# Gated DeltaNet stage: the order of work in its projection loop, and block products of 64x64 and 32x32 in two merge levels

## Chip, core and metric

The kernel runs on one core of a Trainium2 chip. The metric is the device time of one launch in microseconds (us). A core has a matrix engine (TensorE, "PE"), a vector engine (VectorE, "DVE"), a scalar engine (ScalarE, "ACT"), GpSimd ("POOL") and a queue engine (SyncE, "SP") that issues most loads. Each runs its own program in order; they meet at semaphores. PE writes to PSUM, eight banks of 128 partitions by 512 fp32.

## What is computed

Two decoder layers on 256 tokens of width 1024. Each layer is an FFN, a token mixer and a second FFN, so there are six stages: FFN, sliding-window attention, FFN, FFN, gated DeltaNet, FFN. The change is in the fifth. Cut to what matters, it is:

```python
q, k, v = split(silu(causal_depthwise_conv(qkv, conv_w)))     # 8 heads of 128
# per chunk, with gcum the running sum of the log decay
decay = exp(where(causal, gcum[..., :, None] - gcum[..., None, :], -inf))
a_mat = eye + where(strict, (k @ k.T) * decay * beta[..., :, None], 0)
sol   = triangular_solve(a_mat, concat([v * beta, k * beta * exp(gcum)]), lower=True)
v_new = u - w @ state                                         # u, w = split(sol)
out   = (q * exp(gcum)) @ state + where(causal, (q @ k.T) * decay, 0) @ v_new
```

The kernel uses chunks of 128 tokens, two of them, and inverts the unit triangular 128x128 matrix of each head and chunk: 16 matrices.

## The kernel before

**Stages and units.** Weights come in units of 2048 fp32 per partition. SP loads a unit into one of three slots, ACT rounds it to a high part (`hi`), DVE subtracts to get the low part (`lo`), and PE multiplies with three products (high x high, high x low, low x high). A unit can be rounded when PE has used the unit three before it. The DeltaNet stage has 21 units: 0 to 16 for the projection, 17 to 20 for the output projection.

**Projection loop.** Every engine has a hand-written loop over `s` up to 16 (`PROJ_UNITS = 17`). At step s PE multiplies unit s for the first 128 tokens (`wide(s, 0, ...)`) and then for the second (`wide(s, 1, ...)`), 12 matmuls each. Two steps make a chunk `c` of 512 columns: 1 and 2 are k, 3 and 4 q, 5 and 6 v, 7 and 8 z (the output gate). Between these halves lies the side work:

- `rows_of(c, t)` (ACT) copies a chunk's rows out of PSUM, `turn_chunk(c)` (PE) transposes them, `first_tap(c)` (ACT) and `conv(c)` (DVE) make the convolution, `channels(c)` (ACT) the SiLU.
- `turn_back(c)` (PE) transposes k and v back, and for q sums squares; `q_sums(c)` (DVE) copies these sums out. `turn_back(5)` waits until `q_sums(4)` has run and `turn_back(6)` until `channels(6)` has; DVE and ACT reach those calls only after what stands before them in their own loops.
- `decay(b)`, `kk(b)`, `n_of(b)` make the strict lower part N of batch b (b is four heads of one chunk of tokens, 0 to 3); `kq(b)`, `p_of(b)` make the masked q k product.
- `pack(b)` (ACT), `diagonal()`, `solve()`, `spread()` (DVE) and `unpack()` (ACT) collect the 16x16 blocks on the diagonals of all matrices, invert them (14 pairs of small DVE instructions), and put them back into `Tm` (the inverse) and `Wm` (its transpose).

**Merge levels.** The inverse grows from blocks of 16 to 32, to 64, to 128: three levels of four batches, q = 0 to 11. PE works as a pipeline: at step q it makes y(q) = N times the inverse so far, then the second product wt(q-1) from ACT's copy of y(q-1) (`Dm`), then transposes the renewed `Tm` of q-2 (line 1544), which ACT copies to `Wm` (line 1006). In the first two levels these are whole 128x128 products (line 1347, function `four`), POOL masks N for the level (`masked`, line 606), and DVE subtracts the result from the whole of `Tm` (line 1974). The last level has 64x64 products (lines 1515 and 1529) without mask or transpose. Batches 0 to 3 start level 1, and a batch returns four steps later. Between the subtractions DVE makes the low parts of units 17 to 19 in halves (line 1597). After the last level comes `vn0p`, the first product with the finished inverse.

An fp32 product shows in the trace as two records, a transpose as one.

## Time and profile before

| | us |
|---|---|
| time, median of 3 runs (lowest to highest) | 1054.11 (1052.15 to 1054.48) |
| the profiled execution: its time | 1052.97 |
| the profiled execution: its span | 1051.2 |
| PE busy in the span | 1016.9 (97%) |
| DVE, ACT, POOL busy | 610.5, 513.8, 130.4 |
| mean granted PE clock, share of full speed | 0.995 |

The span is from the first to the last instruction; 1.8 us of the profiled time lie around it. The DeltaNet stage lies at about 661 to 850 us of the span, and step s = 9 of its projection starts at 719.6.

### The profile page before, as it was taken

The numbers are of one execution on the slowest core, as the hardware profiler recorded it, in microseconds if no ns is written. First come the engines' busy times: TensorE is split into PE (matmuls) and PEld (weight loads), VectorE is DVE, ScalarE is ACT, GpSimd is POOL, SyncE is SP. The second block draws the span as 40 slices with busy tenths as digits, with TensorE's granted clock in tenths as the row PEclk, the third lists the DMA queues.
The fourth block names the chain that finished last, engine by engine and source line by source line (L and its number), as shares of the span: only waits on it lengthen the run. The fifth ranks groups of instructions, "written<-read, shape, count | busy, mean of one in ns | idle before, by whom it ended". The sixth has DMA issues, their size and how long they took to land.

```text
span 1051.2 us, 14102 instructions
## 1 busy us (share of the span) xinstructions
PE 1016.9 (97%) x5012; PEld 843.5 (80%) x5012; DVE 610.5 (58%) x743; ACT 513.8 (49%) x714; POOL 130.4 (12%) x239
## 2 busy tenths in 40 slices
PE   7999999998999999999999999999989899999997
PEld 5888888777888888887888888788869778888886
DVE  5654454767574554557454545776866576545544
ACT  6444344555464444446443444687765364444442
POOL 4600000150000000000000000136434310000000
PEclk9999999999999999999999999999989999999999
DMA  9665555361265555555655553553223036555541
GB/s 328 222 199 182 192 185 199 121 220 42 80 219 195 167 199 184 179 183 176 215 172 192 195 195 130 181 195 125 102 99 120 2 120 209 191 199 163 197 160 41
DMA packets 123815, 175.41 MB, mean 167 GB/s; under 512 B 7233, under 2 KB 98562, under 8 KB 123778
## 3 DMA queue, kind: packets, MB, share of 16 engines
q1 hardware_dynamic: 121824, 171.00, 48.1%
q0 software_dynamic: 864, 3.15, 0.9%
q10 hardware_dynamic: 1090, 0.77, 0.2%
q8 instruction: 23, 0.38, 0.1%
q14 instruction: 14, 0.11, 0.0%
HBM read 173.85 MB, written 1.05 MB: 166 GB/s over the span
## 4 chain that ended last, share of the span: by engine, by line
PE 91%; DVE 3%; ACT 3%; issue 2%; DMA 0%; POOL 0%; ACTq 0%; DVEq 0%; POOLq 0%
PE banks L1043 19%; PE banks L1045 18%; PE banks L1044 18%; PE banks L1081 9%; PE banks L1083 9%; PE banks L1088 8%; PE banks L1347 3%; PE banks L1117 2%; DVE xT_low L1610 1%; ACT xT_high L696 1%; PE banks L1061 1%; PE banks L1357 0%; PE banks L1378 0%; PE banks L1254 0%; PE banks L1544 0%
## 5 line engine op out<-in xcount | busy, mean ns | idle before, releaser
L1591 DVE TENSOR_TENSOR w_low<-w_raw,w_high 128x2048 fp32r<-128x2048 f32 x151 | 346.6, 2298 | 214.0 <-ACT w_high L674 186.9
L1043 PE MATMUL banks<-w_high,xT_high 128*128 128x512 f32 (+1 forms) x880 | 350.1, 398 | 7.7 <-DVE xT_low L1610 7.2
L1045 PE MATMUL banks<-w_high,xT_low 128*128 128x512 f32 (+1 forms) x880 | 343.0, 390 | 0.0
L1044 PE MATMUL banks<-w_low,xT_high 128*128 128x512 f32 (+1 forms) x880 | 342.1, 389 | 0.0
L674 ACT ACTIVATE w_high<-w_raw 128x2048 fp32r<-128x2048 f32 x108 | 206.4, 1911 | 113.7 <-PE banks L1088 113.7
L1043 PEld LDWEIGHTS banks<-w_high,xT_high 128*128 128x128 f32 x880 | 166.2, 189 | 44.1 <-DVE xT_low L1610 8.5
L1045 PEld LDWEIGHTS banks<-w_high,xT_low 128*128 128x128 f32 x880 | 165.9, 189 | 35.3
L1044 PEld LDWEIGHTS banks<-w_low,xT_high 128*128 128x128 f32 x880 | 166.3, 189 | 31.8
L1081 PE MATMUL banks<-w_high,hT_high 128*128 128x512 f32 x320 | 124.9, 390 | 0.0
L1083 PE MATMUL banks<-w_low,hT_high 128*128 128x512 f32 x320 | 124.5, 389 | 0.0
L660 ACT ACTIVATE w_high<-w_raw 128x2048 fp32r<-128x2048 f32 x47 | 89.7, 1916 | 24.6 <-PE banks L1045 21.8
L1088 PE MATMUL banks<-w_high,hT_low 128*128 128x512 f32 x320 | 98.5, 389 | 0.0
L775 ACT ACTIVATE mixer_arena<-banks,rstd 128x256 f32<-128x256 f32 x88 | 41.8, 475 | 113.6 <-PE banks L1045 113.6
L780 ACT ACTIVATE hT_high<-banks 128x512 fp32r<-128x512 f32 x40 | 23.9, 598 | 149.7 <-PE banks L1117 149.7
L639 POOL TENSOR_SCALAR pow_base<-y_sumsq 128x1 f32<-128x1 f32 x12 | 3.6, 302 | 738.3 <-ACT squares L708 738.3
L1712 DVE TENSOR_TENSOR hT_low<-banks,hT_high 128x512 fp32r<-128x512 f32 x40 | 27.6, 691 | 81.7 <-ACT hT_high L780 81.7
L1088 PEld LDWEIGHTS banks<-w_high,hT_low 128*128 128x128 f32 x320 | 60.1, 188 | 12.5
L1083 PEld LDWEIGHTS banks<-w_low,hT_high 128*128 128x128 f32 x320 | 60.1, 188 | 12.3
L1081 PEld LDWEIGHTS banks<-w_high,hT_high 128*128 128x128 f32 x320 | 60.1, 188 | 12.3
L1705 DVE SCALAR_TENSOR_TENSOR mixer_arena<-banks,rstd,mixer_arena 128x256 f32<-128x256 f32 x88 | 42.3, 481 | 39.7 <-ACT mixer_arena L775 39.7
L1081 PE MATMUL banks<-w_high,xT_high 128*128 128x512 f32 x96 | 38.9, 406 | 2.1 <-DVE xT_low L1617 1.7
L1083 PE MATMUL banks<-w_low,xT_high 128*128 128x512 f32 x96 | 37.5, 391 | 0.0
(240 smaller groups left out, 900.0 us busy)
## 6 DMA issues: line engine op xcount, KB each, us to landing
w_raw<-in_l_ffn_w_in SPq DMA_DIRECT2D x172, 512.0 KB, 4.6
w_raw<-in_l_ffn_w_out SPq DMA_DIRECT2D x88, 512.0 KB, 3.9
w_raw<-in_b_w_in SPq DMA_DIRECT2D x32, 512.0 KB, 4.4
w_raw<-in_a_w_in SPq DMA_DIRECT2D x10, 512.0 KB, 4.3
w_raw<-in_a_w_out SPq DMA_DIRECT2D x8, 512.0 KB, 4.2
w_raw<-in_b_w_out SPq DMA_DIRECT2D x8, 512.0 KB, 3.8
gain_rows<-in_l_norms POOLq DMA_DIRECT2D x6, 512.0 KB, 4.2
w_raw<-in_l_ffn_w_in SPq DMA_DIRECT2D x8, 256.0 KB, 4.6
```

The costliest lines, as they stand in the source:

```text
L660: act.activation(whi[:, c % 3, 0:n], raw[:, c % 3, 0:n], ACT.Copy).then_inc(w_hi, 1)
L674: act.activation(whi[:, c % 3, :], raw[:, c % 3, :], ACT.Copy).then_inc(w_hi, 1)
L775: act.activation(sg[:, t, :], PS[:, banks[t], 0:FC], ACT.Silu, scale=rstd[:, t:t + 1]).then_inc(silu_done, 1)
L1043: pe.matmul(dst, sh, wh, start=start, stop=False)
L1044: pe.matmul(dst, sh, wl, start=False, stop=False)
L1045: return pe.matmul(dst, sl, wh, start=False, stop=stop)
L1081: pe.matmul(PS[:, 2 * t + h, :], sh[:, k, tok], whi[:, c % 3, cols], start=start and k == 0, stop=False)
L1083: pe.matmul(PS[:, 2 * t + h, :], sh[:, k, tok], wlo[:, c % 3, cols], start=False, stop=False)
L1088: last = pe.matmul(PS[:, 2 * t + h, :], sl[:, k, tok], whi[:, c % 3, cols], start=False, stop=stop and k == 1)
L1347: last = pe.matmul(PS[:, bank, col(i)], lhs(i), rhs(i), start=start, stop=True)
L1591: dve.tensor_tensor(wlo[:, c % 3, :], raw[:, c % 3, :], whi[:, c % 3, :], ALU.subtract).then_inc(w_lo, 1)
L1705: dve.scalar_tensor_tensor(out=gated[:, t, :], in0=PS[:, banks[t], FC:2 * FC], scalar=rstd[:, t:t + 1], in1=sg[:, t, :], op0=ALU.mult, op1 ...
```

## The change

**Order.** PE: `kk(0)` and `kk(1)` move from the middle of step 10 to the end of step 9, `kk(2)` and `kk(3)` from its end to its middle, `turn_back(4)` from the middle of step 12 to its end. ACT: all four `pack` stand in step 10, around `rows_of(5, 1)`; `channels(5)` and `channels(6)` stand ahead of the rounding of units 15 and 17; `unpack` moves from step 14 to the end of step 15. DVE: `q_sums(3)` goes behind `lo(13)`, `lo(14)` ahead of `conv(5)`, `q_sums(4)` ahead of the solve, the solve is cut in two (7 pairs each) with `lo(15)`, `conv(6)` and `lo(16)` between them, `spread` comes last, and the low parts of units 17 and 18 are made at steps 15 and 16; those of unit 19 stay in halves in the merge.

**Merge.** Level 1 (q 0 to 3) multiplies only the two 64x64 blocks on each diagonal, 8 products instead of 4 whole ones, still masked, and still turns `Tm`. Level 2 (q 4 to 7) takes N unmasked and makes only the 32x32 quarters below the diagonal: 8 products for y and 16 for the second step, 8 of which give the same quarter turned, so nothing is transposed; ACT and DVE copy the quarters with the sign changed. Level 3 stays. The wait for z, v and the masked q k products ahead of the merge is cut into waits at the first steps that use their banks.

```diff
@@ ACT, projection loop
                     if s == 11:
                         channels(4)
-                        pack(2)
-                        pack(3)
...
                     if s == 10:
                         pack(0)
                         pack(1)
+                        rows_of(c, 1)
+                        pack(2)
+                        pack(3)
+                    if s == 12:
+                        rows_of(c, 1)
+                        channels(5)
+                    if s == 14:
+                        channels(6)
...
+                    if s == 15:
+                        unpack()
...
-                    if s == 14:
-                        unpack()
-                    if s in (4, 6, 12, 14):
+                    if s in (4, 6):
                         channels(c - 1)
@@ ACT, merge
+                    if q < 4:
+                        act.activation(Dm[:, q % 2, 0:256], PS[:, q % 2, 0:256], ACT.Copy).then_inc(y_cp, 1)
+                    elif q < nq - 4:
+                        act.activation(Dm[:, q % 2, 0:128], PS[:, q % 2, 0:128], ACT.Copy).then_inc(y_cp, 1)
...
+                    elif 6 <= q < 10:
+                        b = (q - 2) % 4
+                        for up_, down_ in PAIRS:
+                            last = act.activation(Wm[up_, 4 * b:4 * b + 4, down_], heads(PS[up_, 2 + q % 2, 0:128]),
+                                                  ACT.Copy, scale=-1.0)
+                        last.then_inc(w_cp, 1)
@@ PE, projection loop
                     if s == 10:
-                        kk(0)
-                        kk(1)
+                        kk(2)
+                        kk(3)
...
+                    if s == 12:
+                        turn_back(4)
                     if s == 9:
+                        kk(0)
+                        kk(1)
                         decay(2)
                         decay(3)
@@ PE, merge
-                pe.wait_ge(z_done, 4)
-                pe.wait_ge(v_done, 4)
-                pe.wait_ge(p_done, 4)
...
+                        if q < 4:
+                            for i in range(HG):
+                                for half in (TOP, LOW):
+                                    last = pe.matmul(PS[half, q % 2, i * 64:i * 64 + 64],
+                                                     heads(NM[:, q % 2, :])[half, i, half], Tm[half, 4 * b + i, half],
+                                                     start=True, stop=True)
+                        elif q < nq - 4:
+                            for i in range(HG):
+                                for up_, down_ in PAIRS:
+                                    last = pe.matmul(PS[down_, q % 2, i * 32:i * 32 + 32],
+                                                     heads(Nm[:, b, :])[up_, i, down_], Tm[up_, 4 * b + i, up_],
+                                                     start=True, stop=True)
...
+                                for up_, down_ in PAIRS:
+                                    y = Dm[down_, r % 2, i * 32:i * 32 + 32]
+                                    w = Wm[down_, 4 * b + i, down_]
+                                    pe.matmul(PS[down_, 4 + r % 2, i * 32:i * 32 + 32], w, y, start=True, stop=True)
+                                    last = pe.matmul(PS[up_, 2 + r % 2, i * 32:i * 32 + 32], y, w,
+                                                     start=True, stop=True)
@@ DVE, projection loop
                     if s == 11:
-                        q_sums(3)
                         diagonal()
                         lo(base + 13, 13)
+                        q_sums(3)
+                        lo(base + 14, 14)
                         conv(5)
-                        lo(base + 14, 14)
-                        solve()
+                        q_sums(4)
+                        solve(1, 8)
                     if s == 12:
-                        q_sums(4)
                         lo(base + 15, 15)
                     if s == 13:
+                        conv(6)
+                        lo(base + 16, 16)
+                        solve(8, B - 1)
                         spread()
-                        lo(base + 16, 16)
-                        conv(6)
                     if s == 15:
                         p_of(0)
+                        lo(base + 17, 17)
+                    if s == 16:
+                        lo(base + 18, 18)
@@ DVE, merge
+                    if r < 4:
+                        for half in (TOP, LOW):
+                            v = Tm[half, 4 * b:4 * b + 4, half]
+                            last = dve.tensor_tensor(v, v, heads(PS[half, 4 + r % 2, 0:256]), ALU.subtract)
```

In `PAIRS` stand the partitions 0 to 31 with 32 to 63, and 64 to 95 with 96 to 127.

**DVE around the end of the solve.** A row is an instruction: line, operation, output and inputs, partitions x elements; the x at the end counts repeats. `COPY gdn_small<-banks` is `q_sums`, `w_low` is `lo`, the first `SCALAR_TENSOR_TENSOR ... 128x255` of a group is the start of `conv`. Before, the last pair of the solve, then `q_sums(4)`, `lo(15)`, `spread` and `lo(16)`:

```order
L1893 TENSOR_TENSOR diag_product<-diag_inverse 128x14
L1895 TENSOR_TENSOR diag_inverse<-diag_inverse,diag_product 128x14
L1826 COPY gdn_small<-banks 128x2x4
L1591 TENSOR_TENSOR w_low<-w_raw,w_high 128x2048
L1902 TENSOR_TENSOR diag_blocks<-diag_inverse,block_mask 128x512
L1904 STREAM_TRANSPOSE diag_blocks<-diag_blocks 128x16x32
L1906 TENSOR_TENSOR diag_blocks<-diag_inverse,block_mask 128x512
L1908 STREAM_TRANSPOSE diag_blocks<-diag_blocks 128x16x32
L1591 TENSOR_TENSOR w_low<-w_raw,w_high 128x2048
```

And now the end of `conv(5)`, `q_sums(4)` and the start of the first half of the solve:

```order
L1881 SCALAR_TENSOR_TENSOR mixer_arena<-banks,conv_w,mixer_arena 128x253 x2
L1867 COPY gdn_small<-banks 128x2x4
L1931 MEMSET diag_inverse 128x16
L1935 TENSOR_TENSOR diag_product<-diag_inverse 128x14
L1937 TENSOR_TENSOR diag_inverse<-diag_inverse,diag_product 128x14
```

`q_sums(4)` has moved from behind all 28 instructions of the solve to ahead of them.

**ACT in steps 14 to 16.** `L660` (now `L661`) is `hi`, `L875` (`L876`) `z_of`, `L923` (`L924`) `unpack`, `L904` (`L905`) `channels`, `L932` (`L933`) `v_rows`. Before, from `hi(17)` on:

```order
L660 ACTIVATE w_high<-w_raw 128x2048
L875 ACTIVATE mixer_arena<-banks,rstd 128x512
L923 ACTIVATE mixer_arena<-diag_blocks 32x16x32 x8
L904 ACTIVATE mixer_arena<-mixer_arena 128x256 x4
L660 ACTIVATE w_high<-w_raw 128x2048
L875 ACTIVATE mixer_arena<-banks,rstd 128x512
```

And now, from `channels(6)` on:

```order
L905 ACTIVATE mixer_arena<-mixer_arena 128x256 x4
L661 ACTIVATE w_high<-w_raw 128x2048
L876 ACTIVATE mixer_arena<-banks,rstd 128x512
L661 ACTIVATE w_high<-w_raw 128x2048
L924 ACTIVATE mixer_arena<-diag_blocks 32x16x32 x8
L876 ACTIVATE mixer_arena<-banks,rstd 128x512
L933 ACTIVATE mixer_arena<-banks 128x512 x2
L876 ACTIVATE mixer_arena<-banks,rstd 128x512
L661 ACTIVATE w_high<-w_raw 128x2048
```

`channels(6)` now stands ahead of `hi(17)`, `hi(18)` and `unpack`, and `unpack` has `z_of(8, 0)`, `v_rows(6)`, `z_of(8, 1)` and `hi(19)` behind it.

## Rows read from the trace of the kernel before

**Rows 1.** Chain that ended last, 760 to 817 us: start, length, piece

```profile
761.65 4.53 issue
766.19 1.94 PE banks L1378 x8
768.12 0.43 PE banks L1043
771.16 0.24 PE banks L1045
791.26 1.01 issue
792.27 4.76 PE banks L1347 x40
801.48 0.44 PE banks L1544 x4
801.92 1.79 PE banks L1347 x16
808.59 0.60 PE banks L1515 x8
816.09 2.05 PE banks L1347 x16
```

**Rows 2.** Windows: bounds, length, busy time per engine, granted clock, DMA share, GB/s

```profile
761.00:766.00 5.00, 0.65 (x6) 0.41 (x4) 4.28 (x22) 1.57 (x4) 0.00 (x0) 0.78 0.45 176
766.00:771.00 5.00, 4.81 (x17) 4.18 (x18) 4.93 (x5) 3.00 (x3) 4.58 (x4) 0.54 0.33 113
813.50:816.00 2.50, 1.90 (x32) 1.63 (x32) 1.21 (x3) 0.64 (x2) 0.00 (x0) 1.00 0.02 7
```

**Rows 3.** Timeline of DVE: start, length, instruction, idle before and releaser

```profile
762.63 0.22 DVE L1893 TENSOR_TENSOR diag_product<-diag_inverse 128x56 f32<-128x56 f32 x1
765.92 0.17 DVE L1826 COPY gdn_small<-banks 128x8 f32<-128x8 f32 x1
768.20 0.68 DVE L1902 TENSOR_TENSOR diag_blocks<-diag_inverse,block_mask 128x512 f32<-128x512 f32 x1
771.26 1.07 DVE L1908 STREAM_TRANSPOSE diag_blocks<-diag_blocks 128x512 f32<-128x512 f32 x1
774.37 4.74 DVE L1840 SCALAR_TENSOR_TENSOR mixer_arena<-banks,conv_w,mixer_arena 128x255 f32<-128x255 f32 x12
789.58 0.69 DVE L1864 TENSOR_TENSOR squares<-banks,squares 128x512 f32<-128x512 f32 x1 [9.88 <-PE banks L1347]
```

**Rows 4.** Timeline of ACT, the same columns

```profile
761.25 1.57 ACT L885 ACTIVATE mixer_arena<-banks,conv_w 128x256 f32<-128x256 f32 x4 [2.11 <-PE banks L1357]
778.22 5.11 ACT L923 ACTIVATE mixer_arena<-diag_blocks 32x512 f32<-32x512 f32 x8
```

**Rows 5.** Timeline of PE: `turn_back(6)`, and the last merge level

```profile
784.74 1.10 PE L1378 MATMUL banks<-ident,mixer_arena 128*128 128x128 f32 x8 [0.85 <-ACT mixer_arena L904]
...
813.77 0.27 PE L1515 MATMUL banks<-mixer_arena,x_gained 64*64 64x64 f32 x1
813.82 0.22 PE L1529 MATMUL banks<-mixer_arena 64*64 64x64 f32 x1
...
814.22 0.22 PE L1529 MATMUL banks<-mixer_arena 64*64 64x64 f32 x1
814.22 0.22 PE L1515 MATMUL banks<-mixer_arena,x_gained 64*64 64x64 f32 x1
```

**Rows 6.** Groups by shape, 724 to 832 us: count, busy us, mean ns, idle before

```profile
L660 ACT ACTIVATE w_high<-w_raw 128x2048 fp32r<-128x2048 f32 x8 | 15.3, 1915 | 6.4 <-PE banks L1045 6.3
L1591 DVE TENSOR_TENSOR w_low<-w_raw,w_high 128x2048 fp32r<-128x2048 f32 x6 | 13.7, 2281 | 0.0
L932 ACT ACTIVATE mixer_arena<-banks 128x512 f32<-128x512 f32 x4 | 2.3, 592 | 4.7 <-PE banks L1378 4.7
L1978 DVE TENSOR_SCALAR mixer_arena<-banks 64x256 f32<-64x256 f32 x4 | 1.7, 417 | 3.4 <-PE banks L1529 3.4
```

More of the change, by code:

```diff
@@ L68 @@
 CT = 3 * GH
-LEVELS = (16, 32)
-NLEV = len(LEVELS) + 1
+LEVELS = (16,)
+NLEV = 3
 B = 16
@@ L973, in gdn @@
                     hi(base + s + 3, s + 3)
-                    if s % 2 == 0 and s != 16:
+                    if s % 2 == 0 and s not in (10, 12, 16):
                         (rows_of if c <= 6 else z_of)(c, 1)
+                    if s == 15:
+                        unpack()
                     if s == 4:
@@ L998, in gdn @@
                         act.wait_ge(wt_ps, q - 1)
-                    if q < nq - 4:
-                        act.activation(Dm[:, q % 2, :], PS[:, q % 2, :], ACT.Copy).then_inc(y_cp, 1)
+                    if q < 4:
+                        act.activation(Dm[:, q % 2, 0:256], PS[:, q % 2, 0:256], ACT.Copy).then_inc(y_cp, 1)
+                    elif q < nq - 4:
+                        act.activation(Dm[:, q % 2, 0:128], PS[:, q % 2, 0:128], ACT.Copy).then_inc(y_cp, 1)
                     else:
                         act.activation(Dm[LOW, q % 2, 0:256], PS[LOW, q % 2, 0:256], ACT.Copy).then_inc(y_cp, 1)
-                    if 2 <= q < nq - 2:
+                    if 2 <= q < 6:
                         b = (q - 2) % 4
@@ L1459, in gdn @@
                     if s == 10:
-                        kk(0)
-                        kk(1)
+                        kk(2)
+                        kk(3)
                     if s == 11:
                         turn_back(3)
-                    if s == 12:
-                        turn_back(4)
                     if s == 14:
@@ L1506, in gdn @@
                             pe.wait_ge(wt0_done, 2)
+                        if q < 2:
+                            pe.wait_ge(z_done, q + 2)
                         if q >= 4:
@@ L1510, in gdn @@
                             pe.wait_ge(y_cp, q - 1)
-                        if q < nq - 4:
-                            last = four(q % 2, lambda i: NM[:, q % 2, col(i)], lambda i: Tm[:, 4 * b + i, :])
+                        if q < 4:
+                            for i in range(HG):
[9 more added lines that the diff above has]
+                                                     start=True, stop=True)
                         else:
@@ L1532, in gdn @@
                         else:
+                            if r < 2:
+                                pe.wait_ge(v_done, r + 3)
                             if r >= 4:
-                                pe.wait_ge(w_cp, r - 3)
-                            last = four(4 + r % 2, lambda i: Wm[:, 4 * b + i, :], lambda i: Dm[:, r % 2, col(i)])
+                                pe.wait_ge(w_cp, r - 1)
+                            for i in range(HG):
+                                if r < 4:
+                                    for half in (TOP, LOW):
+                                        last = pe.matmul(PS[half, 4 + r % 2, i * 64:i * 64 + 64],
+                                                         Wm[half, 4 * b + i, half], Dm[half, r % 2, i * 64:i * 64 + 64],
+                                                         start=True, stop=True)
+                                    continue
+                                for up_, down_ in PAIRS:
[3 more added lines that the diff above has]
+                                    last = pe.matmul(PS[up_, 2 + r % 2, i * 32:i * 32 + 32], y, w,
+                                                     start=True, stop=True)
                         last.then_inc(wt_ps, 1)
-                    if 2 <= q < nq - 2:
+                    if 2 <= q < 6:
                         r = q - 2
@@ L1540, in gdn @@
                         pe.wait_ge(wt_done, r + 1)
+                        if r == 0:
+                            pe.wait_ge(z_done, 4)
+                        if r == 1:
+                            pe.wait_ge(p_done, 4)
                         if r >= 2:
@@ L1885, in diagonal, with solve @@
                                                   op0=ALU.mult, op1=ALU.add))
-                def solve():
-                    dve.memset(dinv[:, 0:B * B:B + 1], 1.0)
-                    for j in range(1, B - 1):
+                def solve(j0, j1):
+                    if j0 == 1:
+                        dve.memset(dinv[:, 0:B * B:B + 1], 1.0)
+                    for j in range(j0, j1):
                         n = B - 1 - j
@@ L1971, in gdn @@
                     dve.wait_ge(wt_ps, r + 1)
+                    if r < 4:
+                        for half in (TOP, LOW):
+                            v = Tm[half, 4 * b:4 * b + 4, half]
+                            last = dve.tensor_tensor(v, v, heads(PS[half, 4 + r % 2, 0:256]), ALU.subtract)
+                        last.then_inc(wt_done, 1)
+                    elif r < nq - 4:
+                        for up_, down_ in PAIRS:
+                            last = dve.tensor_scalar(Tm[down_, 4 * b:4 * b + 4, up_],
+                                                     heads(PS[down_, 4 + r % 2, 0:128]), -1.0, None, ALU.mult)
+                        last.then_inc(wt_done, 1)
                     if r < nq - 4:
-                        v = Tm[:, 4 * b:4 * b + 4, :]
-                        dve.tensor_tensor(v, v, heads(PS[:, 4 + r % 2, :]), ALU.subtract).then_inc(wt_done, 1)
-                        if r < 6:
-                            lo_half(base + 17 + r // 2, 17 + r // 2, r % 2)
+                        if r < 2:
+                            lo_half(base + 19, 19, r)
                     else:
```

7 lines of the change are left out of this document (2 added, 5 removed).

## The prediction

> **What bounds the kernel now.** PE is busy 97% of the span, so I read the chain that ended last, and in it the places where PE stands still. In the DeltaNet stage there are three [rows 1]. The longest: PE finishes the transposes of chunk 6 and from 761.65 stands still for 4.53 us before `turn_back(5)` (line 1378). The chain calls this "issue". The cause is in DVE's timeline: `q_sums(4)` runs at 765.92, behind the whole solve, and PE starts at 766.19 [rows 3]. What follows is slow too. The granted clock is 0.78 in the stretch with the standstill and 0.54 in the next 5 us, the lower of PE's two levels (1.2 instead of 2.4 GHz) for most of it [rows 2], and a wide matmul takes 0.43 us instead of 0.24 [rows 1]. The second place is the start of `turn_back(6)` at 784.74: PE waited 0.85 us for `channels(6)` [rows 5], which stands behind `unpack`, eight copies of 5.11 us in all [rows 4]. The third is 1.01 us ahead of the merge, on which DVE's last `p_of` ends [rows 1].
>
> The merge itself runs from 792.27 to 816.09, 23.82 us. In its first two levels PE never rests: the pattern 0.44 (four transposes) and 1.79 (two whole products of four heads) repeats, 2.23 us a step [rows 1]. The third level waits on copies between engines.
>
> **The order, part by part.** `q_sums(4)` now stands ahead of the solve: 4.53 us go. The slow clock follows that standstill and nothing else in the stage, so I let it go too: 8 transposes take 1.94 instead of 0.87 (1.07), and the six wide matmuls up to 770.7 take 0.43 instead of 0.24 (1.2), together 2.3 [rows 1]. `channels(6)` ahead of `unpack` takes 0.85. The waits ahead of the merge are cut up, and DVE's `p_of` is needed only at later steps: 1.01. Sum: 4.53 + 2.3 + 0.85 + 1.01 = 8.7 us, so y(0) can start at 783.6.
>
> What is late next? I followed the four queues forward with the durations of the trace.
> - `turn_back(5)` needs `channels(5)`, which needs `conv(5)`. With `lo(14)` (2.28) ahead of it [rows 6], `conv(5)` ends at about 757 and `channels(5)` at 757.5; PE is there at 761.5, 4 us later.
> - On DVE, `conv(6)` starts when ACT's taps come, at about 762.2 [rows 4]. Then 4.74 for it, 2.28 for `lo(16)`, 3.3 for the second half of the solve (762.63 to 765.92) and 4.1 for `spread` (768.20 to 772.33): 776.6 [rows 3, 6]. PE needs unit 16 at about 774; its low part is there at 769.2. The low parts of units 14 and 15 are ready 10 and 6 us early.
> - ACT does `unpack` until about 781.3. PE needs it at 783.6, so the 5.11 us stay covered, with 2.3 to spare. But `z_of`, two `v_rows`, `z_of` and `hi(19)` stand behind it, four copies of about 0.6 and 1.9 for `hi(19)`, less overlaps about 4 us [rows 6]: ACT is free at 785.3, and PE waits for the first copy of the merge. That is a new wait of about 1.2 us.
> - `lo(17)` and `lo(18)` fall into the 9.88 us in which DVE had nothing to do [rows 3] and end at 781.6, just when PE has made the next product for `p_of`. They cost nothing; if they end later, `p_of(3)` still has until 789. SP can load units 20 and on sooner.
> - `kk(0)` and `kk(1)` a half step earlier only swap places with `decay(2)` and `decay(3)`. They hold ACT's queue 1.8 us longer at 730, and `hi(13)` now stands behind all four `pack`; even so the low parts of units 12 and 13 come 2.5 and 5 us before PE needs them.
>
> **The merge.** The price of one record decides. A 64x64 product alone in its quarter of the array: eight records in 0.60 us, tile-size change included [rows 1]; I take 0.060 each and 0.12 for the change. When two streams use opposite quarters, each keeps about 0.064 (813.77 to 814.22 for eight records of line 1515), and the other stream's records fall between: 0.033 per record for both together [rows 5]. In level 1 the halves TOP and LOW alternate on opposite quarters, so I take 0.033. The 32x32 product is not in the trace. Its bounds are 0.033 and 0.060; half the columns speak for the lower end, two products in a row on the same rows for the upper. I take 0.045.
>
> Level 1: 16 records for y (0.53 + 0.12), 16 for wt (0.53), four transposes (0.44 + 0.12): 1.74 us of PE a step. Level 2: 16 x 0.045 + 0.12 and 32 x 0.045 = 2.3 a step; the transposes at its start belong to level 1. Level 3 as before, 0.6 per group. Summed over the 24 groups and four transposes this is 2.6 + 2.1 + 3.4 + 5.8 + 5.0 + 2.2 = 21.1 us of PE. To it come waits: 1.2 at the first copy, about 0.4 where DVE has two subtractions of 0.42 each and half a `lo` (1.2) in one step [rows 6], about 0.4 where wt(4) and wt(5) wait for ACT's `Wm` copies (partly gone when PE is slower), 0.7 at the end: some 2.1 to 2.7, so 23.2 in all. The merge gains 0.6 us at this price. With 0.033 for the 32x32 records it takes 21.45 and gains 2.4; with 0.060 it takes 25.9 and loses 2.1.
>
> Sum: 8.7 + 0.6 = 9.3 us, with 11.0 and 6.6 at the two ends. Everything after `vn0p` (816.09) just moves. From the profiled time, 1052.97 - 9.3 = 1043.7. The median of the runs lay 1.1 above the profiled one, so I say 1044.0.
>
> **A rule that speaks against it.** In rows 5 the two streams write different banks (line 1515 banks 0 and 1, line 1529 banks 2 and 3). In the new level 1 both halves of a product pair write the same bank, in other partitions, and no row shows that. The Trainium skill, "TensorEngine Tiling (Array Packing)", Restrictions and Gotchas, says that different row tiles cannot access the same PSUM bank at the same time. By that rule the halves would take turns; this is rival 1. The same page, Performance Considerations, gives each matmul an overhead of some 60 cycles, so that short ones stop getting cheaper; no row here shows it below 64 columns. As an estimate from that page, two passes of 60 cycles at 2.4 GHz make 0.05 us a record at 32 columns, and by it the sum would be about 8.5.
>
> **Rivals.**
> 1. *The halves take turns.* Every small record costs 0.060, as line 1515 alone does. Followed through the queues the merge takes 28.4 us, 4.6 more than before, and the sum is 8.7 - 4.6 = 4.1: 1048.9. Against it: nothing but the partitions' being different. If the 32x32 ones are cheap even so (0.033), it is 8.8: 1044.2.
> 2. *The clock falls in the merge.* The long light stretch is new: some 20 us of small products. For it: the clock did fall once [rows 2]. Against it: in 813.5 to 816 PE was busy 1.90 of 2.5 us with 64x64 products and kept 1.00 [rows 2]. If it falls for 4 to 8 us, the loss is up to half of that, as after the standstill (2.3): 1046 to 1048.
> 3. *The waits only move.* If DVE or ACT is 2 to 4 us later than I followed, PE stands at `turn_back(5)` or at the first copy of the merge; 1045.5 to 1047.5, more if the clock goes with it.
> 4. *Slower: a small product costs as much as a whole one.* The two levels now have 320 small records where they had 128 whole ones at 1.79 / 16 = 0.11 [rows 1]. At 0.11 each the merge takes 44.4 us, 20.6 more, and the sum is 11.9 us of loss: 1064.9. It turns at 0.074 a record, where the merge costs what the order gives. Rows 1 and 5 show 0.06 and 0.033 at 64x64, so only the 32x32 ones could do it, from about 0.09 each on (192 of the 320 are theirs).
>
> **How the numbers follow.** My forecast (1042 to 1046.5) 0.55, rival 1 0.17, rival 2 0.12, rival 3 0.11, rival 4 0.05. The range takes in the low end 1052.97 - 11.0 = 1042.0 less 0.7 for run to run, and the cases 1 to 3: 1041.3 to 1049.5. A measurement tells about 0.2% (2.1 us). Of the cases only the fourth lies above 1056.2, and only parts of 3 and 4 reach within 2.1 of no change: faster 0.94, same 0.02, slower 0.04.
>
> **What would show it.** No standstill of PE between the transposes of chunk 6 and `turn_back(5)`, and the clock at 1.00 from 760 to 775. y(0) near 783.6 us, 8.7 earlier than before. A wait of about 1.2 us for the first `Dm` copy, behind `hi(19)`. Level 1 records 0.03 us apart if halves overlap, 0.06 if rival 1 holds. `vn0p` near 807. The prediction is wrong if PE stands for over 1 us in steps 12 to 16, if the clock falls after 785, or if a 32x32 record takes over 0.06.

## The result, and the profile after

The changed kernel took 1046.29 us in the median of 10 runs (1045.04 to 1050.17), the kernel before in the same comparison 1054.47 (1052.06 to 1057.31). The ratio is 0.9931, 95% interval 0.9918 to 0.9944: 0.7% faster and 8.2 us in the medians, where 9.3 and a time of 1044.0 were predicted. The profiled run took 1045.29 us with a span of 1043.5 (before 1051.2). Its mean granted clock, 0.995, is not the usual one: eight of the ten runs have 0.985 to 0.990, and so has a second profile of the same kernel, e13 below (0.990).

The windows come first. The columns are bounds, length, busy time of PE with its records, granted clock, share of DMA, GB/s.

```profile
755.00:760.00 5.00, 5.00 (x30) 1.00 0.64 240
760.00:765.00 5.00, 5.00 (x32) 1.00 0.00 0
...
785.00:790.00 5.00, 2.99 (x83) 1.00 0.99 356
790.00:795.00 5.00, 4.12 (x92) 1.00 0.28 74
795.00:800.00 5.00, 3.56 (x171) 1.00 0.54 187
800.00:805.00 5.00, 4.16 (x57) 0.51 0.01 3
805.00:810.00 5.00, 4.49 (x26) 0.50 0.00 0
810.00:815.00 5.00, 5.00 (x43) 0.97 0.01 3
```

Where the kernel before stood still at a clock of 0.78 and then 0.54 [rows 2], PE is busy at 1.00. But the new merge, from 785.06 on, leaves PE without work for 4.3 of the 15 us to 800, and from 800 to about 810 the clock is at its lower level. Rows 2 had 1.00 up to 816.

The timeline of PE (start, length, line, tiles, count, idle before and its releaser):

```profile
754.93 1.92 PE L1387 MATMUL banks<-ones,mixer_arena 128*128 128x1 f32 x16 [0.62 <-POOL mixer_arena L557]
762.30 1.03 PE L1372 MATMUL banks<-ident,mixer_arena 128*128 128x128 f32 x8
763.17 1.04 PE L1393 MATMUL banks<-ident,mixer_arena 128*128 128x128 f32 x8
...
785.06 1.15 PE L1527 MATMUL banks<-mixer_arena 64*64 64x64 f32 x32
788.20 0.68 PE L1563 MATMUL banks<-mixer_arena 64*64 64x64 f32 x16 [1.99 <-ACT mixer_arena L1007]
...
797.71 0.41 PE L1533 MATMUL banks<-mixer_arena,x_gained 32*32 32x32 f32 x15
797.93 0.18 PE L1570 MATMUL banks<-mixer_arena 32*32 32x32 f32 x1
798.20 0.19 PE L1571 MATMUL banks<-mixer_arena 32*32 32x32 f32 x1
...
800.68 0.21 PE L1571 MATMUL banks<-mixer_arena 32*32 32x32 f32 x1 [1.26 <-issue]
804.29 0.31 PE L1552 MATMUL banks<-mixer_arena 64*64 64x64 f32 x1
...
806.85 5.65 PE L1362 MATMUL banks<-mixer_arena 128*128 128x128 f32 x32 [0.51 <-DVE mixer_arena L2032]
```

- `turn_back(5)` (line 1393) stands right behind `turn_chunk(6)` (line 1372): the 4.53 us of rows 1 are gone.
- `turn_back(4)` waits 0.62 for POOL, new.
- y(0) starts at 785.06. The first wt waits 1.99 us for ACT's `Dm` copy.
- Level 1 (lines 1527 and 1563): 32 records in 1.15 us, 16 in 0.68; less the 0.22 that a record runs [rows 5], that is 0.030 and 0.031 apart, though both halves write the same bank.
- Level 2: 15 records of y in 0.41 us, 0.016 apart (one runs 0.19); the 32 of wt start within 0.27 us (797.93 to 798.20), under 0.009 apart.
- Behind the record of 799.22 PE stops for 1.26 us in the middle of such a group, waiting for no engine.
- Level 3 runs at the lower clock: a record lasts 0.31 instead of 0.22 [rows 5].
- `vn0p` comes at 806.85 (before 816.09 [rows 1]).

How the runs are compared: the profiles reach this stage up to 4 us apart, since in some of them (e2, e3, e5, e8, e12) the clock is low once for 3 to 10 us in an earlier stage, from about 256 on. So I count from `turn_chunk(4)` (727.88 before, 728.74 after).

| | y(0) | `vn0p` | from `vn0p` to the span's end |
|---|---|---|---|
| before | 64.39 | 88.21 | 235.1 |
| after | 56.32 | 78.11 | 236.6 |
| gain | 8.07 | 10.10 | -1.5 |

10.10 less 1.5 less the 0.86 by which the stage began later is 7.7, the difference of the spans.

### The profile page after: what moved, and what is told of

It reads as the page before. It is cut to its first block, busy times and chain, and to the rows that moved or that the text cites. A ratio compares the mean times of both kernels' runs of the same rounds, so it can differ in the third digit from the quotient of the medians.

```text
span 1043.5 us, 14457 instructions
## 1 busy us (share of the span) xinstructions
PE 1010.7 (97%) x5188; PEld 837.0 (80%) x5188; DVE 612.4 (59%) x749; ACT 510.9 (49%) x718; POOL 122.4 (12%) x232
## 4 chain that ended last, share of the span: by engine, by line
PE 87%; DVE 8%; ACT 4%; issue 1%; DMA 0%; POOL 0%; ACTq 0%; DVEq 0%; POOLq 0%
PE banks L1058 18%; PE banks L1060 17%; PE banks L1059 17%; PE banks L1096 9%; PE banks L1098 9%; PE banks L1103 9%; PE banks L1132 2%; DVE xT_low L1651 1%; PE banks L1362 1%; DVE w_low L1632 1%; DVE mixer_arena L1881 1%; ACT xT_high L697 1%; PE banks L1076 1%; ACT mixer_arena L924 0%; DVE diag_inverse L1937 0%
## 5 line engine op out<-in xcount | busy, mean ns | idle before, releaser
L1632 DVE TENSOR_TENSOR w_low<-w_raw,w_high 128x2048 fp32r<-128x2048 f32 x153 | 351.9, 2303 | 214.0 <-ACT w_high L675 186.9
L661 ACT ACTIVATE w_high<-w_raw 128x2048 fp32r<-128x2048 f32 x47 | 89.7, 1918 | 22.3 <-PE banks L1060 19.2
L1103 PEld LDWEIGHTS banks<-w_high,hT_low 128*128 128x128 f32 x320 | 60.1, 188 | 12.5
L1098 PEld LDWEIGHTS banks<-w_low,hT_high 128*128 128x128 f32 x320 | 60.1, 188 | 12.3
L1096 PEld LDWEIGHTS banks<-w_high,hT_high 128*128 128x128 f32 x320 | 60.1, 188 | 12.3
```

The source lines that it names most:

```text
L661: act.activation(whi[:, c % 3, 0:n], raw[:, c % 3, 0:n], ACT.Copy).then_inc(w_hi, 1)
L1096: pe.matmul(PS[:, 2 * t + h, :], sh[:, k, tok], whi[:, c % 3, cols], start=start and k == 0, stop=False)
L1098: pe.matmul(PS[:, 2 * t + h, :], sh[:, k, tok], wlo[:, c % 3, cols], start=False, stop=False)
L1103: last = pe.matmul(PS[:, 2 * t + h, :], sl[:, k, tok], whi[:, c % 3, cols], start=False, stop=stop and k == 1)
L1632: dve.tensor_tensor(wlo[:, c % 3, :], raw[:, c % 3, :], whi[:, c % 3, :], ALU.subtract).then_inc(w_lo, 1)
```

## Experiments

Every kernel below is the changed one with the edit shown. The table has all twelve; y(0), `vn0p` and the rest are counted as above, and the last column names the stretches of the DeltaNet stage in which the clock was at its lower level, in us of the span.

| kernel | median us | ratio to before [95%] | y(0) | `vn0p` | rest | clock low in |
|---|---|---|---|---|---|---|
| e1_order_only | 1050.11 | 0.9964 [0.9949, 0.9979] | - | 82.57 | 235.5 | 756-760 |
| e2_merge_only | 1052.73 | 0.9994 [0.9978, 1.0010] | 63.89 | 84.09 | 237.6 | 769-772, 803-820 |
| e3_filled | 1044.97 | 0.9916 [0.9896, 0.9936] | 57.92 | 79.86 | 235.2 | 758-762 |
| e4_hi19_late | 1045.29 | 0.9926 [0.9906, 0.9945] | 57.89 | 77.64 | 236.4 | 758-761, 799-809 |
| e5_level2_whole | 1047.10 | 0.9939 [0.9917, 0.9961] | 57.93 | 81.93 | 235.2 | 759-763 |
| e6_twice | 1048.52 | 0.9954 [0.9936, 0.9972] | 57.91 | 82.04 | 237.3 | 757-760, 798-815 |
| e8_channels4 | 1049.79 | 0.9964 [0.9950, 0.9977] | 56.31 | 80.94 | 237.7 | 789-796, 803-816 |
| e9_three | 1042.58 | 0.9909 [0.9890, 0.9928] | 56.31 | 77.39 | 235.2 | none |
| e10_four_edits | 1043.64 | 0.9916 [0.9892, 0.9940] | 55.46 | 77.43 | 235.2 | 787-790 |
| e11_masks_late | 1046.06 | 0.9932 [0.9911, 0.9953] | 57.90 | 79.05 | 237.0 | 757-760, 798-811 |
| e12_no_turned | 1045.82 | 0.9919 [0.9895, 0.9943] | 57.91 | 78.08 | 237.6 | 761-764, 802-815 |
| e13_after_again | 1045.58 | 0.9928 [0.9907, 0.9948] | 57.91 | 78.86 | 237.0 | 757-760, 798-811 |

### Order and merge apart

**e1_order_only**: the merge of the kernel before, with the split waits.

```diff
-LEVELS = (16,)
+LEVELS = (16, 32)
...
-                        if q < 4: ... 64x64 ... elif q < nq - 4: ... 32x32
+                        if q < nq - 4:
+                            last = four(q % 2, lambda i: NM[:, q % 2, col(i)], lambda i: Tm[:, 4 * b + i, :])
```

> The changed order of the projection loop and the split waits, with the merge of the kernel before (whole 128x128 products, masks, transposes in two levels); only the low parts of unit 19 are made in the merge. Theory A (the split as the two traces show it): y(0) comes 7.2 us earlier (792.27 before, 785.06 after), the first copy of the merge costs a wait of about 1.3 us behind hi(19), the merge is otherwise 23.8 us as before, and no clock falls behind it. Gain 5.5 to 6.5 us, ratio 0.9938 to 0.9948. Theory B (the split of the prediction): 8.7 of order less 1.3 for the first copy, 7.4 us, ratio about 0.993, the same as the whole change; then the small products give nothing.

**e2_merge_only**: the projection loops, the low parts and the waits of before, with the new merge.

```diff
-                        if q < 2:
-                            pe.wait_ge(z_done, q + 2)
...
-                        if r < 2:
-                            lo_half(base + 19, 19, r)
+                        if r < 6:
+                            lo_half(base + 17 + r // 2, 17 + r // 2, r % 2)
```

> The new merge alone, behind the projection loop of the kernel before; the low parts of units 17 to 19 are made in halves in six merge steps, as before. Theory A (the light merge itself takes the clock down): granted clock near 0.5 within 15 us of y(0), vn0p about 3 to 4 us earlier than before counted from y(0), 1.5 of it given back behind; gain 1.5 to 3 us, ratio 0.997 to 0.9985, order and merge then add up to the whole (about 8). Theory B (the merge gains 0.6 us, the prediction's number): ratio 0.9994, clock 1.00. Theory C (the fall of the clock in the whole change is a late effect of the projection's order): the clock stays at 1.00 here and the gain is over 3.5 us.

The order alone gained 0.36%, less than either theory. In its profile (1047.28 us) `vn0p` came 5.6 us nearer (88.21 to 82.57), as A had it, but its ten times go from 1047.1 to 1051.6. The five of 1050.96 and more have a mean granted clock of 0.992 or 0.993 where the three shortest have 0.997, so they lose it to the clock (4 to 5 us, an estimate from the two clocks); in which stretch, no trace shows. The merge alone gained nothing that can be measured (0.06%). That is B's time, but by A's mechanism: `vn0p` came 4.1 nearer, the clock fell, and 2.5 were given back behind. C is out.

Windows of e2:

```profile
795.00:800.00 5.00, 4.39 (x108) 1.00 0.02 3
800.00:805.00 5.00, 3.72 (x88) 0.79 0.61 213
805.00:810.00 5.00, 4.93 (x142) 0.50 0.77 235
810.00:815.00 5.00, 4.49 (x41) 0.50 0.56 188
815.00:820.00 5.00, 5.00 (x26) 0.50 0.00 0
```

So the light merge takes the clock down without the new order, and here without any stop inside a group. The parts make 0.36 + 0.06, the whole 0.69%, with intervals of 0.13 to 0.16% either way. That together they are worth more than apart is hardly shown: the three intervals together leave about 0.25% for the 0.27% between.

### Is it PE's idle time in levels 2 and 3?

**e3_filled**

```diff
+                    if 4 <= q <= 12:
+                        for i in range(2):
+                            pe.matmul(PS[:, 6, col(i)], ident[:], ident[:], start=True, stop=True)
```

> The whole change, and at the end of each of the merge steps 4 to 12 two useless whole 128x128 products of the identity with itself into a free bank: 18 products, 36 records, about 4 us of PE work, most of it where PE has nothing to do. Theory A (the clock falls because PE rests in levels 2 and 3, and the stop of 1.26 us at 799.2 belongs to the change of the clock): granted clock 1.00 up to vn0p and behind, no stop of a microsecond inside a group of 32x32 records, vn0p no later than in the whole change, the half clock behind it gone: 1.5 to 3.5 us faster than the whole change, ratio 0.990 to 0.992. Theory B (the stop is PE running out of fetched instructions, since the 32x32 records go by at 0.008 us each, and the clock falls after that stop): a stop of about a microsecond within a group of 32x32 records as before, clock near 0.5 behind it, and the fillers cost up to 2 us: ratio 0.993 to 0.995.

Its windows, columns as above:

```profile
795.00:800.00 5.00, 4.50 (x132) 1.00 0.66 202
800.00:805.00 5.00, 4.56 (x118) 1.00 0.05 14
805.00:810.00 5.00, 5.00 (x60) 1.00 0.00 0
```

And in its timeline of PE:

```profile
802.78 0.18 PE L1571 MATMUL banks<-mixer_arena 32*32 32x32 f32 x1 [0.44 <-issue]
```

With 36 useless records the clock stays at 1.00 through the merge, and from `vn0p` to the end it takes 235.2 us, as before. A is right on the clock. It is wrong on the stop, of which 0.44 us remain at a full clock (B), and on `vn0p`, which it did not expect later. Up to `vn0p` the fillers cost 1.0 us (79.86 against 78.86 in e13), behind it they bring 1.8. The median is 0.6 to 1.3 us below the whole change, within the intervals.

**e5_level2_whole**: level 2 as in e1, level 1 with 64x64 products.

> The whole change with level 2 undone: whole 128x128 products with masked N, transposes and a full subtraction there, as before; level 1 keeps its 64x64 products. Theory A (the 32x32 quarters bring the fall of the clock and the stop, and pay for their saving with it): level 2 takes 2.23 us a step again, the clock stays at 1.00 from 785 to the end of the stage, there is no stop, and the time is within 1.5 us of the whole change, ratio 0.992 to 0.9945. Theory B (quarters save their PE time in full): four steps of 2.23 against about 1.2, 4 us slower than the whole change, ratio 0.997.

Its windows:

```profile
795.00:800.00 5.00, 4.65 (x50) 1.00 0.44 108
800.00:805.00 5.00, 5.00 (x48) 1.00 0.30 105
805.00:810.00 5.00, 4.65 (x52) 1.00 0.00 0
```

There is no stop, and no fall of the clock in the merge. `vn0p` is 3.1 us later than in e13 (81.93, 78.86), the part behind it 1.8 us shorter, 1.3 us in all: theory A. The 32x32 quarters save 3 us and lose over half of it through the clock. Both e3 and e5 still have the waits of level 1, and e4 below, without those waits, has the fall, so it is PE's idle time in levels 2 and 3 that takes the clock down.

### The stop inside a group

**e6_twice**

```diff
                                     last = pe.matmul(PS[up_, 2 + r % 2, i * 32:i * 32 + 32], y, w,
                                                      start=True, stop=True)
+                                for up_, down_ in PAIRS:
+                                    ... the same two products again
```

> The whole change, with the 32 small records of the second product in each of the four steps of level 2 issued twice (same values, same places): 128 more records of 32x32. Theory A (the stop of 1.26 us in the profile of the whole change, and of 0.44 in that with fillers, is PE running out of instructions, which small records use up at 0.008 us each): stops within the doubled groups that are not waits for an engine, together 1.5 to 4 us, ratio 0.995 to 0.997. Theory B (the stop belongs to the change of the clock): at most one such stop, where the clock changes, and 128 x 0.008 = 1 us more work, most of it where PE waits anyway: ratio 0.993 to 0.994.

**e12_no_turned** leaves out the second product of each pair, the turned quarter, so level 3 works with an old one.

```diff
-                                    last = pe.matmul(PS[up_, 2 + r % 2, i * 32:i * 32 + 32], y, w,
-                                                     start=True, stop=True)
```

> The whole change without the 64 small records that make the turned quarter in level 2 (so the later levels work with a wrong transpose): 16 records a step in the second product instead of 32. Theory A (the stop comes from PE using up its instructions): with a third of level 2's records gone there is no stop of over 0.2 us inside a group of 32x32 records, while the clock falls as before or sooner, since PE has less to do. Theory B (the stop is the clock's change): a stop of 1 to 2 us stays. Time 1 to 1.5 us below the whole change by A, the same by B.

Timeline of PE in e6:

```profile
800.38 0.21 PE L1570 MATMUL banks<-mixer_arena 32*32 32x32 f32 x1 [1.35 <-issue]
803.77 0.21 PE L1571 MATMUL banks<-mixer_arena 32*32 32x32 f32 x1 [0.38 <-issue]
```

and in its DMA, windows 797 to 798 and 801 to 802 (queue, packets, MB, share of 16 engines):

```profile
q8 instruction: 1, 0.02, 6.7%
...
q8 instruction: 1, 0.02, 6.0%
```

With the group doubled the time is A's (0.9954), and there are two stops, 1.73 us together: one at the head of the third group of second products, one inside the fourth. With a third of the records gone (e12) there is none, while the clock falls as before: `vn0p` is 0.8 us nearer than in e13, and 0.6 of it is lost behind, so A has the stop right and the time wrong (1045.82, and 1045.58 in e13).

The clock is not the cause. In e13, windows and timeline of PE,

```profile
795.00:800.00 5.00, 4.18 (x169) 0.76 0.57 185
...
800.52 0.20 PE L1571 MATMUL banks<-mixer_arena 32*32 32x32 f32 x1 [0.38 <-issue]
```

it is down from 797.7 on, 2.5 us before the stop, in e11 2.2 and in e6 1.2 us before; in e3, e9 and e10 the stop comes at 1.00, and in e2 and e12 the clock falls and there is no stop. So neither makes the other.

The number of small records is not it either. Counted in the timelines from the first record of y(0), the stop stands behind 335 records of PE in eight of the nine profiles that have one, and behind 336 in e6, whose second one stands behind 463. Without fillers that is 183 small records into level 2, with fillers 167. It is a place in PE's program. And each of the ten stops ends 2.2 to 2.8 us after a packet of the instruction queue has started (798.36 and 800.68 in the changed kernel), whether it lasts 0.16 us (e9), 0.38 to 0.66 (e3, e10, e11, e13), 1.26 to 1.35 (the changed kernel, e6) or 1.69 and 1.96 (e8, e4). The two profiles with 32x32 products and no stop pass the same place 3.4 (e2) and 6.2 us (e12) after the start of such a packet. That fits PE having used up its instructions and waiting for the next block: the small records only bring it to that place early. What sets the start of the packet no row shows.

### The waits ahead of the merge

**e8_channels4**

```diff
-                    if s == 11:
-                        channels(4)
...
                         rows_of(c, 1)
+                        channels(4)
                         pack(2)
                         pack(3)
```

> The whole change, with ACT's channels(4) ahead of pack(2) instead of behind pack(3) and the rounding of unit 13. Theory A (the new order delays channels(4) by 3 us, so that POOL's squares for q end 0.62 us after PE wants them; this wait and the light one-column products behind it take the clock down for some 3 us in most runs): no wait ahead of turn_back(4), clock 1.00 from 750 to 765, y(0) 0.6 to 2.2 us nearer to chunk 4's transposes than in the whole change, 0.7 to 2 us faster in the median, ratio 0.991 to 0.9925. Theory B (that wait is used elsewhere, the dip has another cause): packs and the low part of unit 13 come later, DVE passes it on to q_sums(4); ratio 0.993, the dip stays.

What the new order does at `turn_back(4)`: POOL's squares in the timeline of before,

```profile
744.86 2.89 POOL L556 TENSOR_TENSOR mixer_arena<-mixer_arena 128x256 f32<-128x256 f32 x4 [6.95 <-ACT mixer_arena L904]
```

in that of after, with DVE's `lo` beside them,

```profile
748.36 6.42 POOL L557 TENSOR_TENSOR mixer_arena<-mixer_arena 128x256 f32<-128x256 f32 x4 [7.80 <-ACT mixer_arena L905]
748.39 2.73 DVE L1632 TENSOR_TENSOR w_low<-w_raw,w_high 128x2048 fp32r<-128x2048 f32 x1
```

and in that of e8:

```profile
746.43 2.94 POOL L557 TENSOR_TENSOR mixer_arena<-mixer_arena 128x256 f32<-128x256 f32 x4 [5.11 <-ACT mixer_arena L905]
```

In after they start 3.5 us later (2.6 counted from `turn_chunk(4)`), behind four `pack`, and take 6.42 us instead of 2.89, since DVE makes two low parts at the same time. PE waits 0.62, then has the light one-column products. The clock then fell in eight of nine profiles with this order and wait (the exception is the first one of the whole change) and in none of the three without the wait (e8, e9, e10); that costs 1.6 us (y(0) at 57.9 instead of 56.3). The Trainium skill, "GPSIMD Engine Reference", Specifications, has GpSimd share its interfaces with VectorE and contend with DVE instructions that have two SBUF inputs. The rows agree: 2.2 times as long beside `lo`, which has two.

e8 removes wait and dip (y(0) 56.31), and yet it takes 318.5 us from `turn_chunk(4)` to the end, e13 315.9, and its ratio is 0.9964. Its timeline of PE:

```profile
785.82 1.44 PE L1526 MATMUL banks<-mixer_arena 64*64 64x64 f32 x32 [0.79 <-issue]
790.11 1.12 PE L1562 MATMUL banks<-mixer_arena 64*64 64x64 f32 x16 [2.85 <-ACT mixer_arena L1006]
```

and its windows:

```profile
785.00:790.00 5.00, 1.39 (x33) 0.90 0.68 239
790.00:795.00 5.00, 4.89 (x72) 0.50 0.55 184
```

PE comes 1.6 us earlier than in e13, ACT's first `Dm` copy does not (60.1 us after `turn_chunk(4)`, 59.9 in e13), since `unpack` there waits 2.60 us for DVE's `spread`: y(0) waits 0.79, the first wt 2.85, and PE is busy for 1.39 of 5 us. The clock falls at once, and again in level 2. A is right on the wait and the first dip; on the time both theories failed.

**e4_hi19_late**

```diff
-                    hi(base + s + 3, s + 3)
+                    if s < 16:
+                        hi(base + s + 3, s + 3)
...
+                hi(base + 19, 19)
                 for hg in range(NG):
                     act.wait_ge(c3["s1p"], hg + 1)
```

and `lo(base + 19, 19)` behind the two `new_values(0, ...)` on DVE.

> The whole change, with the high part of unit 19 made by ACT behind the last merge step (it stood ahead of the merge) and its low part by DVE behind the two new values of vn0p (it stood in halves in merge steps 0 and 1). Theory A (the wait of 1.3 to 2.0 us ahead of wt(0) is ACT's rounding of unit 19, the waits of 0.39 and 0.50 ahead of the first transposes are DVE's halves): all three go, vn0p is 2 to 2.9 us nearer to the start of chunk 4's transposes than the 78.1 of the whole change, the clock falls in level 2 as there: about 2 us faster, ratio 0.991. Theory B (the rounding is hidden work wherever it stands, or a gap is only passed on): DVE's step of two subtractions or the tail takes the gain, ratio 0.993, the clock falls earlier since PE rests as long elsewhere.

The three waits (1.99 or 1.29, 0.39, 0.50) are gone. Against e13 `vn0p` is only 1.2 us nearer and against the first profile 0.5, where A had 2 to 2.9, since the stop is 1.96 here:

```profile
799.75 0.21 PE L1573 MATMUL banks<-mixer_arena 32*32 32x32 f32 x1 [1.96 <-issue]
```

The time, 0.9926, is not to be told from the whole change. A is right on the waits, and on the time neither can be chosen.

**e11_masks_late**

```diff
                         pool.wait_ge(chan_done, 24)
+                        pool.wait_ge(unpacked, 2)
```

> The whole change with one more wait: POOL masks N for the merge only when DVE has finished spread. Theory A (POOL's masks slow DVE's solve): the two solve instructions at 771.8 and 773.0 take 0.21 instead of 1.2 us, spread and unpack come 2 us earlier, the wait ahead of wt(0) shrinks from 1.3 or 2.0 us to under 0.5: 1 to 2 us faster than the whole change, ratio 0.9915 to 0.993 with the clock's fall in the merge unchanged. Theory B (the slow instructions are slow for another reason, or the masks now come too late for y(0) and y(1)): no gain or 1 us of loss.

Timelines of after, POOL's masks and DVE's solve:

```profile
769.99 4.14 POOL L607 TENSOR_TENSOR mixer_arena<-x_gained,level_masks 128x512 f32<-128x512 f32 x2 [5.18 <-issue]
771.76 1.19 DVE L1937 TENSOR_TENSOR diag_inverse<-diag_inverse,diag_product 128x56 f32<-128x56 f32 x1
772.99 1.21 DVE L1935 TENSOR_TENSOR diag_product<-diag_inverse 128x54 f32<-128x54 f32 x1
```

and of e11, the first of the same two instructions, ACT's `hi(18)` and `unpack`, DVE's two `lo`:

```profile
771.52 0.22 DVE L1938 TENSOR_TENSOR diag_inverse<-diag_inverse,diag_product 128x56 f32<-128x56 f32 x1
776.77 1.92 ACT L662 ACTIVATE w_high<-w_raw 128x2048 fp32r<-128x2048 f32 x1 [2.95 <-PE banks L1061]
778.60 5.10 ACT L925 ACTIVATE mixer_arena<-diag_blocks 32x512 f32<-32x512 f32 x8
779.17 6.51 DVE L1633 TENSOR_TENSOR w_low<-w_raw,w_high 128x2048 fp32r<-128x2048 f32 x2
```

A's cause is right: the masks cost the solve 2.0 us. Nothing is won: `unpack` stands behind `hi(18)`, which waits for PE, and starts at 778.60 as it did at 778.68 (there it had waited 0.58 us for DVE, in e13 not at all); and the masks now slow the two `lo` (6.51 instead of 4.48). 0.9932: B on the time.

### Several edits together

**e9_three**: e4, e8 and the fillers of e3.

> Three edits on the whole change together: channels(4) earlier, unit 19 rounded behind the merge, and two useless whole products at the end of merge steps 4 to 12. If each removes its own loss (0.62 to 2.2 us at turn_back(4), about 2.5 at the merge's start, the half clock of 10 us in level 3 and behind it, 2 to 3): 4.5 to 6 us faster than the whole change, ratio 0.9875 to 0.989. If they only pass a gap on to one another: 2 us, ratio 0.991.

**e10_four_edits**: e9 with e11's wait, fillers in steps 4 to 8 only.

> The three edits of e9_three (channels(4) ahead of pack(2), unit 19 rounded behind the merge, useless whole products), with the useless products only at the end of merge steps 4 to 8, and a fourth: POOL masks N for the merge only when DVE has finished spread. Theory A (POOL's two masks at 770 take 2.0 us from DVE's solve, 1.20 instead of 0.21 for two of its instructions, and spread, unpack, the z copies and the first copy of the merge stand in a row behind it): y(0) no longer waits 0.78, the wait of 1.05 ahead of wt(0) is under 0.2, the fillers in level 3 cost nothing now, the clock stays at 1.00: 1.5 to 3 us faster than e9_three's profile (1041.9), 1039 to 1040.5, 6 us faster than the whole change. Theory B (the clock falls in level 3, now without fillers, or the masks are late for y(0)): 1042 to 1044.

**e13_after_again**: no edit.

> The whole change once more, unedited, on the same chip as the three others, so that their times have it beside them. Both theories: ratio 0.993. In its profile the clock may fall in 755 to 760 (1.6 us), which it did in three of four kernels with the same order there, and not in the first profile of this one; in the merge it falls.

Windows of e9:

```profile
785.00:790.00 5.00, 3.69 (x98) 1.00 0.99 350
790.00:795.00 5.00, 5.00 (x129) 1.00 0.20 70
795.00:800.00 5.00, 4.84 (x148) 1.00 0.02 7
```

Its timeline of PE:

```profile
786.46 0.68 PE L1564 MATMUL banks<-mixer_arena 64*64 64x64 f32 x16 [1.05 <-ACT mixer_arena L1007]
```

Timeline of PE in e10:

```profile
786.84 1.12 PE L1529 MATMUL banks<-mixer_arena 64*64 64x64 f32 x16 [1.93 <-POOL mixer_arena L608]
```

In e9 the clock stays at 1.00 from 740 to 830. From `turn_chunk(4)` to the end it takes 312.5 us, the whole change 314.8 and 315.9. Its median, 1042.58, is 3.0 us below that of e13 and its ratio the lowest of all, but the intervals (0.9890 to 0.9928, and 0.9907 to 0.9948) overlap: probably 2 to 3 us better than the whole change, about half of the 4.5 to 6 expected. In e10 `unpack` comes earlier, and now y(1) waits 1.93 us for POOL's mask. The clock falls behind that wait (787 to 790). It ends where e9 does (312.6), and its median, 1043.64, is B's. In level 3, now without fillers, the clock kept 1.00, so in this kernel they were not needed there.

## Why the prediction was right, and where it was not

The time lies in the range. Of the three signs that were to show the prediction wrong one came, the clock fell after 785; the other two did not (PE never stood over 1 us in steps 12 to 16, no 32x32 record took 0.06). So the mechanism is right in the main for the order of work, and for the merge the number is right by luck, as the terms show.

- **Standstill and slow clock behind it (4.53 + 2.3).** Right: `turn_back(5)` follows directly and the clock is 1.00 from 760 to 775.
- **`channels(6)` (0.85) and the wait ahead of the merge (1.01).** Right, both gone. From `turn_chunk(4)` to y(0) it takes 8.07 us less in the first profile; 8.7 were predicted. The 0.62 at `turn_back(4)` is the difference: the step that failed is the one that followed the queues with the durations of before. It had POOL's squares at 2.89 us and `channels(4)` free of the moved `pack`. In the other profiles the clock fell behind this wait too, and the gain was 6.5 (64.39 to 57.91).
- **First `Dm` copy, 1.2 us.** 1.99 and 1.29 were measured; e4 shows the cause, `hi(19)`. The 4 us from `unpack` to the copy were right (783.8 to 787.75).
- **`unpack` covered with 2.3 us to spare.** Mis-sized: it ended at 783.8 instead of 781.3. Two things hold it, and the prediction had neither: `hi(18)`, ahead of it in ACT's queue and waiting for PE, ends at 778.1 (778.7 in e13, where nothing else holds it), and the solve took 2 us more beside the masks, which adds 0.58 in the first profile.
- **Level 1 records at 0.033.** Measured 0.030 and 0.031. Rival 1, that the halves take turns in one bank, is refuted (0.060). The Trainium skill, "TensorEngine Tiling (Array Packing)", Restrictions and Gotchas, says that different row tiles cannot access the same PSUM bank at the same time. For these products, which write one bank in different partitions, the rows do not bear it out.
- **32x32 records at 0.045, bounds 0.033 and 0.060.** Mis-sized, and outside the bounds: 0.016 in y, under 0.009 in wt. In y half the columns cost half of what a 64x64 record does (0.016, 0.031), where the lower bound was the whole. The argument for the upper end, two products in a row on the same rows, shows no cost at all in wt. 64 x 0.016 + 128 x 0.009 is 2.2 us of PE, where the sum had 192 x 0.045 = 8.6.
- **The merge, 23.2 us.** It took 21.8 and 20.95 (e13), with less work and more waiting than in the sum. (Its 5.0 us for level 3 are 4.8 at its own price of 0.6 for each of eight groups.)
- **"Everything after `vn0p` just moves."** Failed: it took 1.5 and 1.9 us longer, as the clock is low there. The sum had this loss at nothing. Rival 2 (chance 0.12), the fall of the clock, came true beside the forecast, not in its place: the clock was low for 10 and 14 us. e3 and e5 show that PE's idle time in levels 2 and 3 does it. The argument against it was one row of rows 2 (1.90 of 2.5 us busy, 1.00), which followed a fully busy stretch [rows 1]; the new merge has 2.99, 4.12 and 3.56 of 5 us in a row.
- **Rival 3.** Came true in part: 0.62 at `turn_back(4)`, up to 0.8 more than 1.2 at the first copy. **Rival 4** is refuted by the record prices.

Sum for e13: 6.5 (order, with its dip) + 2.9 (merge: 23.82 to 20.95) - 1.9 (behind it) = 7.5, the difference of the spans (1051.2 to 1043.7). 8.7 + 0.6 were predicted. Merge and clock together made 1.0 in e13 and 0.5 in the first profile, close to the 0.6, but from a gain of 2.9 or 2.0 and a loss of 1.9 or 1.5: two errors that cancel. In the same way `vn0p` at 806.85, near the 807 forecast, is a start 1.5 us late and a merge 1.4 us short.

Open: why the clock did not fall at 755 to 760 in the first profile, and what sets the start of the instruction packet.

## What to carry over

Work taken off PE in a stretch where it waits for copies buys little: here PE was without work for 4.3 us of 15, and the clock went down for 10 us. Follow a new order with the durations that instructions have beside their new neighbours, above all DVE's two-input subtractions beside POOL. And a wait removed ahead of a light stretch can cost more than it brings (e8): look at who is next and at how busy PE stays.

## What the hardware showed that I had not expected

- 32x32 fp32 records (two a product) start 0.016 us apart in y, which uses two places of the array in turn, and under 0.009 in wt, which uses four. The Trainium skill, "TensorE: Matmul & The Clock Gate", Wait — 56ns, not 53.3ns?, says that start to start never drops below about 25 ns however small the product. Per record these rows go below it; per product, y has 0.031 and wt under 0.018.
- PE can stop for 0.2 to 2.0 us, with no engine to wait for, at one place of its program: behind 335 records from y(0) in nine profiles (336 in e6), and in e6 again 127 records on. Each of the ten stops ends 2.2 to 2.8 us after the start of an instruction packet; the two profiles that come to the place 3.4 and 6.2 us after one have no stop.
- POOL's products take 2.2 times as long beside DVE's `lo` (6.42, 2.89), and two solve instructions over 5 times as long beside POOL's masks (1.20, 0.22).
